# A two-block transformer forward on one core: router weights as the stationary operand, the memory's load and norm moved into an output projection, one norm moved under the memory's keys

## The reference, cut to what matters

```
# first block
aff = softmax(h @ router_w)              # h: 512 x 1024 (normed), router_w: 1024 x 16
w_sel, idx = top_k(aff.T, 64)            # 64 tokens for each of 16 experts
...                                      # gather, three matrices of each expert, scatter-add
# second block
h = h + concat([y_pool, y_dn]) @ w_out           # y_dn from the gated delta rule
m = rmsnorm(mem, mem_norm_g)                     # mem: 256 x 1024
q, k, v = rmsnorm(h, norm_xattn_g) @ w_q, m @ w_k, m @ w_v
h = h + softmax(q k' / 16) v @ w_o
```

## Time and profile before

| | us |
|---|---|
| median of 3 runs | 3014.95 (3013.53 to 3019.21) |
| the profiled execution, time | 3018.05 |
| its span | 3016.3 |
| PE busy in it | 2861.5 |

### The profile page before, as it was taken

The page is one execution under the profiler, slowest core; times in us unless marked ns, Lnnn a source line. Parts: engine busy times, 40 slices in busy tenths (PEclk is TensorE's granted clock), DMA queues, the critical chain, the costliest instruction groups (busy, mean ns, idle before and its releaser), DMA issues.

```text
span 3016.3 us, 27524 instructions
## 1 busy us (share of the span) xinstructions
PE 2861.5 (95%) x10958; PEld 1486.0 (49%) x10958; DVE 871.3 (29%) x1729; ACT 523.8 (17%) x882; POOL 0.2 (0%) x4
## 2 busy tenths in 40 slices
PE   7999999998899999998799999989898999999998
PEld 3566656666644444443444334334594844444444
DVE  3143443433444444212211111155362022110001
ACT  1111111111233333210100000132222121000000
POOL 0000000000000000000000000000000000000000
PEclk9999999999999999999799999999999999999999
DMA  8611111100111111133599999822003403222220
GB/s 311 216 49 51 46 52 52 49 28 28 36 42 56 42 56 49 55 85 126 218 409 409 409 409 409 343 74 70 15 1 98 126 14 87 76 75 75 77 76 35
DMA packets 326928, 372.13 MB, mean 123 GB/s; under 512 B 9953, under 2 KB 272822, under 8 KB 323510
## 3 DMA queue, kind: packets, MB, share of 16 engines
q1 hardware_dynamic: 326480, 370.77, 35.7%
q10 hardware_dynamic: 358, 0.11, 0.0%
HBM read 368.75 MB, written 2.10 MB: 123 GB/s over the span
## 4 chain that ended last, share of the span: by engine, by line
PE 91%; DVE 4%; DVEq 2%; ACT 1%; issue 1%; DMA 1%; ACTq 0%; SPq 0%
PE psum L1660 15%; PE psum L606 13%; PE psum L1572 11%; PE psum L2359 7%; PE psum L1178 7%; PE psum L1313 4%; PE psum L1279 4%; PE psum L597 3%; PE psum L918 2%; PE psum L1465 2%; PE psum L677 2%; PE psum L2159 2%; PE psum L1498 2%; PE psum L1108 2%; PE psum L1157 1%; PE psum L1137 1%
## 5 line engine op out<-in xcount | busy, mean ns | idle before, releaser
L606 PE MATMUL psum<-arena 128*128 128x512 f32 (+1 forms) x1152 | 461.3, 553 | 3.0 <-DVE arena L504 2.9
L1660 PE MATMUL psum<-arena 128*128 128x512 f32 (+1 forms) x1088 | 445.0, 569 | 4.0 <-DVE arena L494 4.0
L1572 PE MATMUL psum<-arena 128*64 128x512 f32 x1536 | 347.6, 597 | 3.0 <-issue 2.1
L1660 PEld LDWEIGHTS psum<-arena 128*128 128x128 f32 x1088 | 206.5, 190 | 241.2 <-issue 236.2
L606 PEld LDWEIGHTS psum<-arena 128*128 128x128 f32 x1152 | 216.3, 192 | 212.6 <-issue 202.4
L1178 PE MATMUL psum<-arena 128*128 128x512 f32 x512 | 233.1, 597 | 0.0
L2359 PE MATMUL psum<-arena 128*128 128x512 f32 x512 | 220.4, 591 | 1.9 <-DVE arena L2376 1.9
L1572 PEld LDWEIGHTS psum<-arena 128*64 128x64 f32 x1536 | 104.9, 136 | 217.5 <-issue 214.4
L2359 PEld LDWEIGHTS psum<-arena 128*128 128x128 f32 x512 | 96.7, 189 | 125.7 <-issue 125.7
L1178 PEld LDWEIGHTS psum<-arena 128*128 128x128 f32 x512 | 92.4, 189 | 104.1 <-issue 104.1
L1503 DVE SCALAR_TENSOR_TENSOR arena<-psum,arena 128x512 f32<-128x512 f32 x64 | 48.0, 751 | 246.6 <-PE psum L1498 246.1
(11 more groups left out here) (309 smaller groups left out, 2738.5 us busy)
## 6 DMA issues: line engine op xcount, KB each, us to landing
arena<-in_w_gate SPq DMA_DIRECT2D x64, 1024.0 KB, 18.4
arena<-in_w_up SPq DMA_DIRECT2D x64, 1024.0 KB, 16.4
arena<-in_w_down SPq DMA_DIRECT2D x64, 1024.0 KB, 18.2
arena<-in_w_in SPq DMA_DIRECT2D x120, 512.0 KB, 3.8
arena<-in_ada_w SPq DMA_DIRECT2D x24, 1024.0 KB, 7.7
arena<-in_w_up SPq DMA_DIRECT2D x32, 512.0 KB, 4.2
arena<-in_w_down SPq DMA_DIRECT2D x32, 512.0 KB, 3.7
arena<-in_w_out SPq DMA_DIRECT2D x16, 512.0 KB, 3.8
```

The costliest lines, as they stand in the source:

```text
L606: mm = pe.matmul(bank[:, 0:b - a], w[:, k, :], HT[:, k, a:b], start=(k == 0), stop=(k == KC - 1))
L1572: mm = pe.matmul(psum[64 * e:64 * e + 64, bank + n, :], tokens(e, 2 * q + k), w[:, k, 512 * n:512 * n + 512], start=(q == 0 and k == 0), s ...
L1660: mm = pe.matmul(psum[:, bank, 0:n], w[:, k, :], x[:, k, :], start=(k == 0), stop=(k == KC - 1))
```

## The change

- **Router.** The router's weights become stationary: 8 matmuls, each with 16 stationary columns and 512 moving columns, block k written to partitions 32 (k mod 4) to 32 (k mod 4) + 15 of bank 5, so that four partial sums lie beneath each other. ACT copies the bank to `row_a`; PE turns it with 4 more transposes, put between the first four and the last four groups of h2T's transposes; DVE adds the four partials in a reduction ahead of the softmax. ACT's exponential moves from after the first copy of h2tok to after the fifth. The bank is zeroed by DVE ahead of the first block's output projection.
- **Memory.** `sp_mem` is gone; ACT issues the load at the delta rule's end (`act_mem_load`, after its last copies of the rule's output, ahead of the roots of its norm). PE's transposes `pe_mem` stand after the first four units of `pe_wout2`, the sum of n_mem after the fifth; DVE copies the memory after the fourth add and scales it after the fifth.
- **Stream's norm.** n_x is numbered after n_mem. ACT's squares of it come after n_mem's root, DVE's six folds after the last add, PE's sum between the keys and the values, ACT's root after the eighth copy in `act_xproj`, DVE's scaling as PE does the values; the queries wait for it.

```
 def pe_router(pe):
     pe.wait_ge(sem("small_in"), 16)
-    for t in range(LT):
-        for k in range(KC):
-            if t == 0:
-                normed(pe, n_ffn, k)
-            mm = pe.matmul(psum[:, 5, t * NE:(t + 1) * NE], h2T[:, k, t * P:(t + 1) * P], router[:, k, :],
-                           start=(k == 0), stop=(k == KC - 1))
+    for k in range(KC):
+        normed(pe, n_ffn, k)
+        j = 32 * (k % 4)
+        mm = pe.matmul(psum[j:j + NE, 5, :], router[:, k, :], h2T[:, k, :], start=(k < 4), stop=(k >= 4))
     mm.then_inc(sem("logits"), 1)
     for n in range(8):
+        if n == 4:
+            pe.wait_ge(sem("logits_out"), 1)
+            for t in range(LT):
+                mm = pe.transpose(psum[:, 7, t * P:(t + 1) * P], row_a[:, t * P:(t + 1) * P], ident)
+            mm.then_inc(sem("logits"), 1)
...
 def act_router(act):
+    act.wait_ge(sem("logits"), 1)
+    act.activation(row_a, psum[:, 5, :], ACT.Copy).then_inc(sem("logits_out"), 1)
     for n in range(8):
...
-        if n == 0:
+        if n == 4:
             act.wait_ge(sem("logits_shifted"), 1)
             act.activation(aff, aff, ACT.Exp).then_inc(sem("aff_exp"), 1)
+def dve_zero_logits(dve):
+    dve.memset(psum[:, 5, :], 0.0)
 def dve_router(dve):
-    dve.wait_ge(sem("logits"), 1)
-    lg = psum[:, 5, 0:LT * NE].rearrange("p (t e) -> p t e", t=LT)
-    dve.tensor_reduce(aff_st[:, :, 0], lg, AX, ALU.max)
+    dve.wait_ge(sem("logits"), 2)
+    parts = psum[:, 7, :].rearrange("p (t j e) -> p t e j", t=LT, j=4)
+    dve.tensor_reduce(aff, parts[:, :, 0:NE, :], AX, ALU.add)
+    dve.drain()
+    dve.tensor_reduce(aff_st[:, :, 0], aff, AX, ALU.max)
...
 def act_dn(act):
...
+    act_mem_load(act)
     for h in range(DNH):
         act.wait_ge(sem("dn_mean"), h + 1)
...
+def act_mem_load(act):
+    act.wait_ge(sem("dn_sums"), LT)
+    act.dma_start(mem_tok, A["mem_2"][0].rearrange("(t p) d -> p t d", p=P)).then_inc(sem("small_in"), 16)
...
+def dve_wout2(dve):
+    dve.sem_inc(sem("w_out2nd_out"), 4)
+    def add(c):
+        done(dve, "w_out2nd", c // 4, c % 4)
+        add_plain(dve, c, psum[:, c % 4, :]).then_inc(sem("w_out2nd_out"), 1)
+    for c in range(4):
+        add(c)
+    dve_mem(dve)
+    add(4)
+    dve_norm(dve, n_mem)
+    for c in range(5, KC):
+        add(c)
+    for k in range(1, KC - 1):
+        dve_fold(dve, n_x, k)
 def pe_wout2(pe):
...
+    pe_mem(pe)
     for u in range(4):
+        if u == 1:
+            pe_norm(pe, n_mem)
         ws.arrived(pe, "w_out2nd", 1, u)
         pe.wait_ge(sem("w_out2nd_out"), 4 + u + 1)
...
-def sp_mem(sp):
-    sp.wait_ge(sem("w_out2nd_out"), 4 + KC)
-    sp.dma_start(mem_tok, ...).then_inc(sem("small_in"), 16)
 def pe_xproj(pe):
     for u in range(8):
         if n >= 2:
             pe.wait_ge(sem("xproj_out"), n - 1)
+        if n < 2:
+            pe.wait_ge(sem("w_out2nd_out"), 4 + 4 + n + 1)
         product(pe, "xk", 0, u, memT, n % 2, C, n_mem if u == 0 else None)
         n += 1
+    pe_norm(pe, n_x)
...
-        product(pe, "xq", 0, u, hx, n % 2)
+        product(pe, "xq", 0, u, hx, n % 2, m=n_x if u == 0 else None)
 def act_xproj(act):
...
             n += 1
+            if n == 8:
+                act_root(act, n_x)
```

More of the change, by code:

```diff
@@ L1393, in act_router @@
                    .then_inc(sem("htok_out"), 1)
-                if n == 0:
+                if n == 4:
                     act.wait_ge(sem("logits_shifted"), 1)
                     act.activation(aff, aff, ACT.Exp).then_inc(sem("aff_exp"), 1)
+        def dve_zero_logits(dve):
+            dve.memset(psum[:, 5, :], 0.0)
         def dve_router(dve):
-            dve.wait_ge(sem("logits"), 1)
-            lg = psum[:, 5, 0:LT * NE].rearrange("p (t e) -> p t e", t=LT)
-            dve.tensor_reduce(aff_st[:, :, 0], lg, AX, ALU.max)
+            dve.wait_ge(sem("logits"), 2)
+            parts = psum[:, 7, :].rearrange("p (t j e) -> p t e j", t=LT, j=4)
+            dve.tensor_reduce(aff, parts[:, :, 0:NE, :], AX, ALU.add)
             dve.drain()
-            dve.tensor_tensor(aff, lg, bcast(aff_st[:, :, 0], NE), ALU.subtract)
+            dve.tensor_reduce(aff_st[:, :, 0], aff, AX, ALU.max)
+            dve.drain()
+            dve.tensor_tensor(aff, aff, bcast(aff_st[:, :, 0], NE), ALU.subtract)
             dve.drain()
@@ L2152, in mixed_block_kernel @@
         w_out2 = cut(A["w_out_2"][0], P)
-        _, dve_wout2 = residual("w_out2nd", 2, [((lambda i, u=u: w_out2[i * 4 + u]),) + unit_place(4 + u) for u in range(4)],
-                                ydT, add_plain, (), [4, 5, 6, 7])
+        ws.phase("w_out2nd", 2, [((lambda i, u=u: w_out2[i * 4 + u]),) + unit_place(4 + u) for u in range(4)], [4, 5, 6, 7])
+        def dve_wout2(dve):
[12 more added lines that the diff above has]
+                dve_fold(dve, n_x, k)
         def pe_wout2(pe):
@@ L2187, in mixed_block_kernel @@
         work3 = spare.take(S)
-        n_x = norm(X2, hx, S, lambda k: vec2[:, XN + k:XN + k + 1], None, 4, work2,
-                   lambda k: ("w_out2nd_out", 4 + k + 1), True)
         xr = Carve(arena, CT_LO, UNIT_LO)
@@ L2202, in mixed_block_kernel @@
                      lambda k: ("mem_out", k + 1), False)
+        n_x = norm(X2, hx, S, lambda k: vec2[:, XN + k:XN + k + 1], None, 4, work2,
+                   lambda k: ("w_out2nd_out", 4 + k + 1), True)
         w_xq, w_xk, w_xo = (cut(A[n][0], P) for n in ("w_xq_2", "w_xk_2", "w_xo_2"))
@@ L2207, in mixed_block_kernel @@
         XSCALE = 256 ** -0.5
-        def sp_mem(sp):
-            sp.wait_ge(sem("w_out2nd_out"), 4 + KC)
-            sp.dma_start(mem_tok, A["mem_2"][0].rearrange("(t p) d -> p t d", p=P)).then_inc(sem("small_in"), 16)
         def pe_mem(pe):
@@ L2422, in N @@
             return lambda e: f(e, m)
-        PE_STEPS = [pe_setup, pe_first, pe_hg, pe_tail, pe_attn, pe_merge, pe_wout, N(pe_norm, n_ffn), pe_router, pe_experts, N(pe_norm, n_fin1), N(pe_norm, n_mix), pe_in2, pe_dn, pe_wout2, N(pe_norm, n_x), pe_mem, N(pe_norm, n_mem), pe_xproj, pe_xattn, pe_xo, N(pe_norm, n_mlp), pe_mlp, N(pe_norm, n_last), pe_last]
-        DVE_STEPS = [dve_setup, dve_mod, N(dve_norm, n_lat), N(dve_norm, n_ctx), dve_hg, dve_tail, dve_attn, dve_merge, N(dve_wout, n_ffn), N(dve_norm, n_ffn), dve_router, dve_experts, N(dve_norm, n_fin1), N(dve_norm, n_mix), dve_in2, dve_dn, N(dve_wout2, n_x), N(dve_norm, n_x), dve_mem, N(dve_norm, n_mem), dve_xattn, N(dve_xo, n_mlp), N(dve_norm, n_mlp), dve_mlp, N(dve_norm, n_last), dve_last]
-        ACT_STEPS = [act_rows, act_setup, act_first, act_hg, act_tail, act_attn, act_merge, N(act_norm, n_ffn), act_router, act_experts, N(act_norm, n_fin1), N(act_norm, n_mix), act_in2, act_dn, N(act_norm, n_x), N(act_norm, n_mem), act_xproj, act_xattn, N(act_norm, n_mlp), act_mlp, N(act_norm, n_last), act_last]
+        PE_STEPS = [pe_setup, pe_first, pe_hg, pe_tail, pe_attn, pe_merge, pe_wout, N(pe_norm, n_ffn), pe_router, pe_experts, N(pe_norm, n_fin1), N(pe_norm, n_mix), pe_in2, pe_dn, pe_wout2, pe_xproj, pe_xattn, pe_xo, N(pe_norm, n_mlp), pe_mlp, N(pe_norm, n_last), pe_last]
+        DVE_STEPS = [dve_setup, dve_mod, N(dve_norm, n_lat), N(dve_norm, n_ctx), dve_hg, dve_tail, dve_attn, dve_merge, dve_zero_logits, N(dve_wout, n_ffn), N(dve_norm, n_ffn), dve_router, dve_experts, N(dve_norm, n_fin1), N(dve_norm, n_mix), dve_in2, dve_dn, dve_wout2, N(dve_norm, n_x), dve_xattn, N(dve_xo, n_mlp), N(dve_norm, n_mlp), dve_mlp, N(dve_norm, n_last), dve_last]
+        ACT_STEPS = [act_rows, act_setup, act_first, act_hg, act_tail, act_attn, act_merge, N(act_norm, n_ffn), act_router, act_experts, N(act_norm, n_fin1), N(act_norm, n_mix), act_in2, act_dn, N(act_norm, n_mem), N(act_squares, n_x), act_xproj, act_xattn, N(act_norm, n_mlp), act_mlp, N(act_norm, n_last), act_last]
         SP_STEPS = [sp_setup] + [lambda e, n=n: ws.load(e, n, sp_mod_late if n == "hg" else None) for n in ws.phases]
@@ L2428, in mixed_block_kernel @@
         SP_STEPS.insert(1 + 1 + 1 + list(ws.phases).index('pool2'), sp_small2)
-        SP_STEPS.insert(SP_STEPS.index(sp_small2) + 7, sp_mem)
         SP_STEPS.append(sp_last)
```

## The result

The changed kernel takes 2993.37 us (median of 4 runs, 2989.43 to 2996.76) where the kernel before takes 3014.24 (4 runs, 3012.27 to 3019.21): 20.9 us less, a ratio of 0.9928 with a 95% interval of 0.9911 to 0.9945. Forecast were 2993.5 us and 21.4 us won; the time lies in the range and is faster by more than the 0.2% that can be told from no change.

The account below looks back on a forecast made before the run. PE was taken as the bound, busy 2861.5 of 3016.3 us. Router 9.9 plus memory and stream's norm 11.5 made 21.4 us won, so 3014.95 became 2993.5 us, range 2989 to 3001.5.

Parts of the forecast that it names:

- Router: From the norm's last block to the gather: 10.9 us won, less three costs, gives 9.9; bounds 5.3 and 11.4.
- The zeroing of the bank: Cost ahead of the first block's output projection: 0.2 us taken, 0.45 if PE's start waits, otherwise 0.
- The gather: Cost at the gather, which starts at 1.2 GHz after PE's idle time: 0.7 us taken, up to 1.7.
- The array's shape: Cost in the router of changing from narrow column groups back to the full array: 0.1 us.
- the sum for full clock: Router's steps after the last norm block at full clock: top-64 at 1441.3 against 1452.66, 11.4 us won.
- The 0.5 that I took off for the clock: In the router, 10.9 us taken, near the upper end between 7.5 (1.2 GHz) and 11.4 (full clock).
- rival 1: Clock stays at 1.2 GHz through the router: 6.5 us won there, 2997 us in all; chance 0.10.
- My bound for 1.2 GHz throughout: Router's products, transposes and softmax all at 1.2 GHz: 7.5 us won.
- the experts pass the gain on: Behind the router: the weight stream has stopped, so its gain arrives in full; gather to experts' end unchanged within 2 us.
- Memory and stream's norm: Second block, ahead of the keys: 20.34 us go, 8.85 come back, 11.5 won; bounds 8.4 and 13.3.
- The covers: Second block: load, roots, scalings and folds cost nothing, hidden under other work; smallest cover left 2.5 us, sixth unit.
- Rival 4: ACT's issue of the memory's load blocks, delaying the delta rule's roots: 3022 us for a 35 us block; chance 0.01.

Follow-up runs that it names:

- the trace with the useless products: Kernel before, plus one unread 512-column product under each of the norm's first seven blocks, against the kernel before: 3014.34 us, ratio 0.9995.

## Why the prediction was right, step by step

- **Router: 9.9 forecast, 10.6 up to the top-64 and 10.5 up to the experts.** The term stood at 10.9 between bounds of 7.5 and 11.4, less 0.1, and 10.6 was measured: from the last block's end (1434.9) to the top-64 it takes 6.3 us, and took 17.0 before (1435.7 to 1452.66). The zeroing of the bank was sized 0.2 and cost 0: PE's projection started as long after DVE's last product of the merge as before. The gather was sized 0.7 and lost 0.1 (9.26 against 9.15). The array's shape: passes start 0.43 apart, the last at 1435.4, and the transposes at 1435.90, under 0.1 us as taken.
- **Where the sum was wrong, and luck covered it.** I read 1435.17 as the moment at which the last norm block is ready. It is the seventh; DVE ends the eighth at 1435.69. The two last shifts of the norm, before and then after the change:

```profile
1434.62 1.07 DVE L504 TENSOR_SCALAR arena<-arena 128x512 f32<-128x512 f32 x2
...
1433.81 1.07 DVE L504 TENSOR_SCALAR arena<-arena 128x512 f32<-128x512 f32 x2
```

  All work behind the last block ran at full clock, so the sum for full clock, 11.4, was the one that applied, and it was 0.8 too high: 0.5 from this start, and 0.2 because the transposes start 1.0 us after the last block and not 0.8. The 0.5 that I took off for the clock was not needed and happened to fill the gap. The misses on the gather and the zeroing (0.9 taken, 0.1 measured) went the other way.
- **The clock.** It was at 0.50 when the sweep began and rose during it, not before (the third column from the right in the stretches below, changed kernel): rival 1 did not come. My bound for 1.2 GHz throughout hid an error. I let blocks 0 to 6 follow the norm at 1.23 us each, but at 1.2 GHz two passes of 512 columns take 1.66 us in one group. They kept pace all the same, because consecutive products are in different column groups, which the sum had not named as its cover. With one group the cover is gone, and the trace shows it, at a cost of 0.85 us.

```profile
1430.00:1432.00 2.00, 2.00 (x6) 0.23 (x4) 1.85 (x5) 0.00 (x0) 0.00 (x0) 0.50 1.02 408
1432.00:1434.00 2.00, 2.00 (x5) 0.14 (x4) 1.85 (x4) 0.00 (x0) 0.00 (x0) 0.84 1.04 416
```

- **That the experts pass the gain on** was right: their length stayed at 473.7 us with the start moved by 1, 11, 16 and 21 us.
- **Memory and stream's norm: 11.5 forecast, 11.6 measured.** Transposes 3.6 forecast and 3.8 measured, sum of n_mem 3.5 and 3.46, sum of n_x 1.75 and 1.72: 8.85 forecast and 8.97 measured. The 0.24 us of the shorter keys, which the sum did not have, make up the rest. DVE's copies set the pace of the transposes as argued: from pair to pair 0.96 us, where 0.82 was taken. The covers held; the smallest, the sixth unit over n_mem's root and scaling, was used to 2298.21 of 2300.8.
- **Rival 4** fell by ACT's queue: 0.41 us.
- **Noise.** I allowed up to 1.7 us for each gap that falls differently against the clock. The traces show more: 5.0 us behind the experts in four of the fourteen. In the profiled execution of the changed kernel luck went the other way: the last products of the attention's values took 3.7 us in place of 5.3, since the clock had not fallen there, and 0.8 us had been won before the change was reached. With these two, the 22.1 us of the terms (10.5 + 11.6) become the 24.5 of the spans; the medians, over four executions each, say 20.9. The 0.5 us between the 21.4 forecast and these 20.9 is smaller than this scatter, so that closeness is luck too; the terms, read from the trace, are what bears the forecast out.

The Trainium skill, TensorE: Matmul & The Clock Gate, section Part 3: Packing small matmuls, says that matmuls whose outputs lie in different 32-partition column groups run at the same time. The traces agree as far as they go: at 1.2 GHz the second product starts 1.66 us after the first in one group, and within the norm's 1.23 in different groups.

## What to carry to other kernels

A burst of matmuls behind a paced producer should have few instructions left when the last block comes, and its moving side should be the long one: from the seventh block on, the same logits took 11.4 us with 16 moving columns (5.6 where the clock was high) and 1.6 with 512, and the clock came up while the second sweep ran. Ahead of a DMA-fed stage ask whether the stream has stopped by the time the stage starts; if it has, time won in front of it arrives whole. When a wait is moved under other work, price what remains of it in PE's own time (here 8.97 us of 20.3), since that is where the next gain lies.

## What the runs showed that was not expected

- During 5.6 us of products with 128 stationary and 16 moving columns, whose records touch one another, the granted clock went from 1.00 to 0.50, at about 1442.4 in the trace with the useless products.
- The same instructions behind the experts can run at a mean clock of 0.77 or 0.94 over 30 us, and need 203.1 or 198.1 us up to the delta rule, even in two traces in which they begin within 0.1 us of each other. A change of 9.4 us ahead of them gave 3.6 us at the end of that trace, and one of 4.7 us gave 4.4.
- Even ahead of the change, in code that is the same, two executions of one and the same kernel reached the sweep of logits at 1423.2 and 1426.95 us. Differences of 3 to 4 us between single executions of this kernel are nothing that a change must explain.
